# A two-layer hybrid attention trunk: first tile in two token halves, memory's turns moved, two-pass head sums, minus |z| on VectorE

## What is computed

```python
def hybrid_layer(x, mem, ...):
    h = rms_norm(x, ln_g)
    u = einsum('bsd,de->bse', h, w_in)           # q, k, v, z of four branches, f, gate logits
    o_sb = stick_breaking_attention(q_sb, k_sb, v_sb)            # 4 heads of 64
    o_fx = forgetting_attention(rms_norm(q_fx), rms_norm(k_fx), v_fx, log_sigmoid(f + b))
    o_dl = dilated_mixture(rope(rms_norm(q_dl)), rope(rms_norm(k_dl)), v_dl)   # 12 heads
    km, vm = split(einsum('bmd,de->bme', rms_norm(mem, mem_ln_g), w_mem_kv))   # 256 memory tokens
    o_mm = memory_cross_attention(rms_norm(q_mm), rms_norm(km), vm)
    y_b = (o_b * silu(z_b)) @ w_br_b             # for each branch b
    merged = sum over b of sigmoid(gate_b) * y_b
    return x + merged @ w_out
```

## Time and profile before

| | us |
|---|---|
| median of 3 runs | 1352.54 |
| lowest and highest | 1352.37, 1352.62 |
| the profiled execution | 1349.81 |
| its span | 1348.0 |
| TensorE busy in it | 1295.9 |
| mean granted TensorE clock | 0.982 |

### The profile page before, as it was taken

How to read it: one execution, slowest core, us unless ns; L and a number is a source line. 1 busy time by engine, 2 the same in 40 slices (tenths; PEclk the granted TensorE clock), 3 DMA queues, 4 the chain that set the end, 5 groups by cost and what they waited for, 6 DMA issues and landing times. The chain is left out here.

```text
span 1348.0 us, 17624 instructions
## 1 busy us (share of the span) xinstructions
PE 1295.9 (96%) x6138; PEld 1022.6 (76%) x6138; DVE 559.3 (41%) x929; ACT 684.1 (51%) x1257; POOL 694.3 (52%) x571
## 2 busy tenths in 40 slices
PE   7998989998999999999999999999999999999998
PEld 6777868875677788887887787787666778888876
DVE  5896253354341322223349945334542313222221
ACT  6665333586444645454456643248745355544531
POOL 4687322364242476777457863125633325767662
PEclk9999989999999999999999998999999999999999
DMA  7545311122222244444364452112222223444432
GB/s 229 157 105 135 97 39 32 48 63 54 54 59 53 66 107 113 107 113 113 98 166 128 118 131 58 39 40 60 59 55 56 55 55 88 114 104 110 105 115 86
DMA packets 209888, 120.79 MB, mean 90 GB/s; under 512 B 9736, under 2 KB 200328, under 8 KB 209800
## 3 DMA queue, kind: packets, MB, share of 16 engines
q1 hardware_dynamic: 209800, 119.66, 33.8%
HBM read 107.04 MB, written 6.29 MB: 84 GB/s over the span
## 5 line engine op out<-in xcount | busy, mean ns | idle before, releaser
L1699 POOL TENSOR_TENSOR w_lo<-w_raw,w_hi 128x512 fp32r<-128x512 f32 (+1 forms) x400 | 498.1, 1251 | 596.0 <-ACT w_hi L1173 547.3
L765 PE MATMUL dense<-h_hi,w_hi 128*128 128x512 f32 x1168 | 496.4, 425 | 5.3 <-POOL w_lo L1699 2.8
L765 PE MATMUL dense<-h_lo,w_hi 128*128 128x512 f32 x1168 | 461.9, 395 | 0.0
L765 PE MATMUL dense<-h_hi,w_lo 128*128 128x512 f32 x1152 | 454.5, 395 | 0.0
L765 PEld LDWEIGHTS dense<-h_hi,w_hi 128*128 128x128 f32 x1168 | 223.0, 191 | 70.1 <-issue 15.8
L1173 ACT ACTIVATE w_hi<-w_raw 128x512 fp32r<-128x512 f32 (+1 forms) x401 | 231.8, 585 | 67.5 <-PE dense L765 66.3
L765 PEld LDWEIGHTS dense<-h_lo,w_hi 128*128 128x128 f32 x1168 | 223.4, 191 | 48.5 <-issue 9.7
L765 PEld LDWEIGHTS dense<-h_hi,w_lo 128*128 128x128 f32 x1152 | 219.7, 191 | 48.5
L1461 DVE TENSOR_TENSOR sig<-dense,x_rstd_row 128x512 f32<-128x512 f32 x48 | 33.2, 692 | 207.7 <-issue 118.4
L1226 ACT ACTIVATE sig<-sig 128x512 f32<-128x512 f32 x48 | 30.3, 632 | 123.2 <-DVE sig L1461 123.2
L1463 DVE TENSOR_TENSOR raw<-dense,x_rstd_row 128x512 f32<-128x512 f32 x80 | 54.9, 686 | 80.8 <-PE dense L765 62.4
(11 more groups left out here) (292 smaller groups left out, 2021.1 us busy)
## 6 DMA issues: line engine op xcount, KB each, us to landing
w_raw<-in_w_in SPq DMA_DIRECT2D x292, 256.0 KB, 2.9
w_raw<-in_w_out SPq DMA_DIRECT2D x32, 256.0 KB, 2.9
x_scratch<-v_dil SPq DMA_DIRECT2D x16, 256.0 KB, 3.5
w_raw<-in_w_mem_kv SPq DMA_DIRECT2D x16, 256.0 KB, 2.8
v_dil<-x_scratch SPq DMA_DIRECT2D x16, 256.0 KB, 2.7
turned<-normed SPq DMA_DIRECT2D x48, 64.0 KB, 2.4
inv_den<-o_norm SPq DMA_DIRECT2D x48, 64.0 KB, 2.4
silu_z<-in_mem SPq DMA_DIRECT2D x4, 512.0 KB
```

What stands on the lines that cost most here:

```text
L765: return nc.tensor.matmul(o, lhsT, rhs, start=start, stop=stop, skip_group_check=True)
L1699: pool.tensor_tensor(w_lo[:, g % SPLIT_SLOTS, c], w_raw[:, g % RAW_SLOTS, c], f(w_hi[:, g % SPLIT_SLOTS, c]), ALU.subtract).then_inc(w_lo_ ...
```

## The change

- The first dense tile of the program runs as eight k-tiles over tokens 0 to 255, then eight over 256 to 511 (`first_tile`), and VectorE's `first_low` and `x_place` are reordered: four lows of half 0, the copies of x tiles 2 and 3, the other four lows of half 0, the eight of half 1.
- `mem_square` moves to the end of the first group; `mem_scale` and the four turns go to the start of the second. Its order is now four full value tiles, then mk 0, v 4, mk 1, v 5, mv 0, z 0, mv 1, z 1. The scaling is done by ScalarE.
- All normed tiles have the square in two parts and two fp32r passes, and they are held back for at least one more tile.
- The second turn of the dilated maxima goes to bank `A1`.
- VectorE forms -|z| as min(-z, z) right behind its copy; ScalarE's Abs goes.
- A stick-breaking step of key tile j is followed by 3 - j free places; six free places at the end of the third group go.

```diff
-ROOM_AT_END = 12
+ROOM_AT_END = 6
@@ scores(SB)
+                if s < len(order):
+                    yield from [("room",)] * (TT - 1 - order[s][1])
@@ dense
-                if waiting[2] and waiting[2][-1].rope:
+                if waiting[2] and waiting[2][-1].normed:
                     add("low", waiting[2][-1])
...
-                while len(waiting[2]) >= lag and not (waiting[3] and waiting[3][-1].rope and waiting[2][0].rope):
+                while waiting[2] and len(waiting[2]) >= max(lag, 1 + waiting[2][0].normed) and not (waiting[3] and waiting[3][-1].rope and waiting[2][0].rope):
@@ plan_layer
-    dense([new(kind, DIL, i) for kind in "qk" for i in range(6)], [("room",), ("x_sum",)] + [("room",)] * 6
-          + [("mem_square",), ("mem_scale",)] + [("mem_t", c) for c in range(4)] + [("room",)] * 2, lag=2)
-    dense([new(*t) for v, t in enumerate((("mk", MM, 0), ("mk", MM, 1), ("mv", MM, 0), ("mv", MM, 1)))
-           for t in (("v", DIL, v), t)] + [new("v", DIL, i) for i in (4, 5)] + pair_of("z", DIL), lag=2)
+    dense([new(kind, DIL, i) for kind in "qk" for i in range(6)], [("room",), ("x_sum",)] + [("room",)] * 13 + [("mem_square",)], lag=2)
+    dense([new(*t) for t in (("v", DIL, 0), ("v", DIL, 1), ("v", DIL, 2), ("v", DIL, 3), ("mk", MM, 0), ("v", DIL, 4),
+                             ("mk", MM, 1), ("v", DIL, 5), ("mv", MM, 0), ("z", DIL, 0), ("mv", MM, 1), ("z", DIL, 1))],
+          [("mem_scale",), ("room",)] + [("mem_t", c) for c in range(4)] + [("room",)] * 18, lag=2)
@@ rings
-                turn_users += [(("max", DIL, 0), max_kept, DIL), (("max", DIL, 1), max_ready, DIL)]
+                turn_users.append((("max", DIL, 0), max_kept, DIL))
+                out_users[2].append((("max", DIL, 1), max_ready, DIL))
@@ square_parts
-            return [part[:, square_ring.slot(t.n), :] for part in (og_dil_hi, og_dil_lo)]
+            i = square_ring.slot(t.n)
+            if t.rope or t.kind == "mk":
+                return [part[:, i, 0:t.width] for part in (og_dil_hi, og_dil_lo)]
+            return [part[:, 4 + i, :] for part in (dq_hi, dq_lo)]
@@ TensorE
+                def first_tile():
+                    for u in range(2):
+                        c = slice(u * MEM, (u + 1) * MEM)
+                        for kt in range(KT):
+                            half, i = divmod(kt, HALF)
+                            if u == 0 and i == 0:
+                                pe.wait_ge(w_lo_ready, half + 1)
+                            pe.wait_ge(first_h_lo[u], kt + 1)
+                            part = slice(i * P, (i + 1) * P)
+                            last = three(dense_bank[0][:, c], w_hi[:, half, part], w_lo[:, half, part],
+                                         h_hi[:, kt, c], h_lo[:, kt, c], u == 0 and kt == 0, u == 1 and kt == KT - 1)
+                            if u == 1 and i == HALF - 1:
+                                last.then_inc(w_used, 1)
...
-                        if t.rope:
-                            pe.wait_ge(*square_lo_ready.of(t.n))
-                            hi, lo = square_parts(t)
-                            mm(o, rc(HEADSUM), hi, start=True)
-                            last = mm(o, rc(HEADSUM), lo, stop=True)
-                        else:
-                            pe.wait_ge(*squared.of(t.n))
-                            last = mm(o, f(rc(HEADSUM)), square[:, square_ring.slot(t.n), 0:t.width], start=True, stop=True)
+                        pe.wait_ge(*square_lo_ready.of(t.n))
+                        hi, lo = square_parts(t)
+                        mm(o, rc(HEADSUM), hi, start=True)
+                        last = mm(o, rc(HEADSUM), lo, stop=True)
...
-                            wait(pe, turn_ring.before(("max", b, order)))
+                            wait(pe, (turn_ring, out_ring[2])[order].before(("max", b, order)))
@@ ScalarE
+                    elif kind == "mem_scale":
+                        act.wait_ge(*mem_rstd.of("exp"))
+                        for i in range(2):
+                            act.activation(mem_tok[:, i, :], mem_tok[:, i, :], ACT.Copy, scale=mem_ms[:, i:i + 1])\
+                                .then_inc(mem_scaled.sem, 1)
...
-                        act.activation(t_, sbz[n % 4][:, w], ACT.Abs).then_inc(z_abs.sem, 1)
                         act.wait_ge(*z_abs.of(key))
-                        act.activation(t_, t_, ACT.Exp, scale=-1.0).then_inc(z_exp.sem, 1)
+                        act.activation(t_, t_, ACT.Exp).then_inc(z_exp.sem, 1)
@@ VectorE
-            first_low(0, 0)
-            first_low(0, 1)
+            for kt in range(HALF):
+                first_low(0, kt)
             x_place(2)
             x_place(3)
             dve.wait_ge(x_placed, 8)
+            for kt in range(HALF, KT):
+                first_low(0, kt)
             for kt in range(KT):
-                if kt >= 2:
-                    first_low(0, kt)
                 first_low(1, kt)
...
                         dve.tensor_copy(sbz[n % 4][:, w], R[score_ring.slot(s)][:, w]).then_inc(z_kept.sem, 1)
+                        dve.wait_ge(*z_kept.of(key))
+                        z = sbz[n % 4][:, w]
+                        dve.scalar_tensor_tensor(out=sbt[n % 2][:, w], in0=z, scalar=-1.0, in1=z, op0=ALU.mult, op1=ALU.min)\
+                            .then_inc(z_abs.sem, 1)
```

More of the change, by code:

```diff
@@ L866, in _ @@
                         t, half, i = s[1:]
+                        if (l, t.n) == (0, 0):
+                            if (half, i) == (0, 0):
+                                first_tile()
+                            continue
                         g = global_item(t.items[half])
@@ L1234, in _ @@
                                        ACT.Square).then_inc(squared.sem, 1)
-                        if t.rope:
-                            act.wait_ge(*squared.of(t.n))
-                            act.activation(square_parts(t)[0], square[:, square_ring.slot(t.n), :], ACT.Copy)\
-                                .then_inc(square_hi_ready.sem, 1)
+                        act.wait_ge(*squared.of(t.n))
+                        act.activation(square_parts(t)[0], square[:, square_ring.slot(t.n), 0:t.width], ACT.Copy)\
+                            .then_inc(square_hi_ready.sem, 1)
                     elif kind == "post2" and s[1].normed:
@@ L1422, in _ @@
                                 .then_inc(out_copied[0], 1)
-                    elif kind == "mem_scale":
-                        dve.wait_ge(*mem_rstd.of("exp"))
-                        for i in range(2):
-                            dve.tensor_scalar(mem_tok[:, i, :], mem_tok[:, i, :], mem_ms[:, i:i + 1], None, ALU.mult)\
-                                .then_inc(mem_scaled.sem, 1)
                     elif kind == "mem_t":
@@ L1515, in _ @@
                         dve.wait_ge(*square_hi_ready.of(t.n))
-                        dve.tensor_tensor(lo, square[:, square_ring.slot(t.n), :], f(hi), ALU.subtract)\
+                        dve.tensor_tensor(lo, square[:, square_ring.slot(t.n), 0:t.width], f(hi), ALU.subtract)\
                             .then_inc(square_lo_ready.sem, 1)
@@ L1610, in _ @@
                             natural = lambda ap: ap.rearrange("p (u r) -> p r u", r=STRIDE)
[L1611 removed]
+                            dve.tensor_tensor(natural(negmax_r[0:NH, :]), A1[0:NH, :].rearrange("p (r u) -> p r u", r=STRIDE),
                                               natural(normed[0:NH, :]), ALU.min).then_inc(max_ready.sem, 1)
```

12 lines of the change are left out of this document (5 added, 7 removed).

## The result

The changed kernel takes 1342.64 us (median of 4 runs, 1339.64 to 1343.98) beside 1352.58 us before: a ratio of 0.9924, 95% interval 0.9910 to 0.9939. It is 9.9 us faster; the forecast of 1313 promised 39.6, and the range ended at 1326. So 29.6 us are missing. The profiled run took 1343.98 us, with a span of 1341.9.

A forecast was written before the change was run, and what follows sets the result against it. The prediction took TensorE's work at its granted clock plus its waits as the bound. Terms of 40.6 us less 1.4 for new waits gave 39.2: 1310.6 for the profiled run, 1313 for the median, range 1303 to 1326.

The forecast's parts named there:

- the head sums' term: Two passes save 6.2 us of matmuls; added copies and subtractions are covered by the lag, which removes 1.6 us of wait.
- the price of the closer rooms: Closer rooms in the dilated columns and later q and k of the third group bring new waits, taken as 1.4 us.
- signs of being wrong: VectorE's chain to negmax_r no shorter, half-clock units still thirteen, or new waits in the value tiles above 5 us.
- First tile: Splitting the first dense tile in two parts lets TensorE start earlier: 1.3 us, bounds 0 to 1.7.
- Memory: Key and value tiles: 12.7 us of waits go, plus 4.7 us from three half-clock units; scaling done 0.4 us before turn 0.
- Maxima: Second turn of the dilated maxima no longer waits for VectorE's copy: 5.2 us in layer 0, 3.7 in layer 1.
- Stick-breaking: Waits for a probability and dk_lo go, net 3.5 us; with the half-clock unit at 976, 5.2 us.
- (3): Rival: the eight half-clock units dropped or hidden turn up elsewhere, six fully paid: 1323 us; chance 0.12.
- (1): Rival: new waits in the value tiles, GpSimd's queue 3 us a layer over its cover, scaling late by 1: 1321; chance 0.14.
- (2): Rival: minus |z| on VectorE contends with GpSimd's reads and lengthens each of 16 steps by 2.3 us: 1355; chance 0.03.
- (4): Rival: more is gained, as four half-clock units after the dilated columns move away (6.6 us): 1306; chance 0.11.
- (5): Rival: waits are not where the change acts, for instance A1 is taken when the maxima come: 1322; chance 0.05.

The follow-up runs named there:

- best three: The kernel before with first tile, memory and maxima together, without the sticks' and head sums' parts: 1328.14 us.
- p_max: The kernel before with only the second turn of the first branch's maxima put into bank A1: 1343.60 us.
- p_stick: The kernel before with only the smaller rooms of the stick-breaking steps and minus |z| on VectorE: 2.3 us slower.
- p_heads: The kernel before with only the head sums in two passes and the lag of the normed tiles: 1362.15 us.
- b_heads: The best three with two passes and lag, Forgetting's gate tiles set between its query tiles, and memory's maxima turned 3 places later: 1331.18 us.
- p_absz: The kernel before with only minus |z| moved from ScalarE to VectorE, rooms as they were: 1352.72 us.
- p_memory: The kernel before with only the value tiles' group order, memory's turns among them and the scaling on ScalarE: 15.8 us faster.
- a_pop: The changed kernel with only one normed tile's second step taken per tile: 1.8 us faster than the changed kernel.
- b_pass_absz: The best three with two passes, no lag, and minus |z| on VectorE: 5.5 us faster than the same without minus |z| there (1350.84 us).
- w_long: The best three with TensorE made to wait at eight places for the gate's last step: 1368.2 us.
- b_memt1: The best three with memory's turns one place further behind the scaling: 1327.52 us.

## Why the prediction was wrong

The step that failed most is the overlap in the head sums' term: the added copies and subtractions, and the lag that was to cover them, were put at nothing, and they cost more than the cheaper matmuls gave (9.7 us lost instead of 7.8 gained). Next is the price of the closer rooms, 1.4 us for all, in the sticks' part (4.9 lost instead of 5.2 gained). Two of the prediction's own signs of being wrong came: more than 5 us of new waits in the value tiles (5.1 for the scaling alone), and a count of half-clock units that didn't fall.

The chain of medians adds up to the missing 29.6 us within 0.3: first tile, memory and maxima 24.5 instead of 27.6 (3.1 short), the sticks' part -4.9 instead of 5.2 (10.1), the head sums' part -9.7 instead of 7.8 (17.5), less the reserve of 1.4 that the forecast had kept back.

**What bounds the kernel.** Right: TensorE is busy for 96 to 97% of the span before, after and in the best three. That work, clock and waits add up to the span is so by construction and shows nothing more.

**First tile.** Not shown to be 1.3. The pair of profiles gives 1.36 us (31.40 to 30.04 for the first head sum), but this mark moves from run to run. In the nine kernels with the old first tile it lies between 29.99 (p_max) and 33.56 us, with a half-clock unit inside the tile in six of them; in the eleven with the new one between 29.61 and 30.34, with no unit. The medians are 31.82 and 29.95. So a gain is likely, and what sets it apart is mostly the unit, which the term didn't have. It wasn't run alone, and memory and maxima alone add up to 25.0 us, more than the 24.5 of the best three, so the medians show nothing of it.

**Memory.** Near in size, 15.8 against 17.4, and partly by luck: of the 12.7 us of waits that were to go, 7.1 went, and what made up the rest isn't shown. The step "0.4 us before TensorE's turn 0" failed: it was 2.5 us after, in both layers. ScalarE's scaling began at 94.43, where TensorE wanted the turn at 94.1, because the square ahead of it waited 1.15 us for VectorE's raw tile; VectorE is late in the key tiles even without memory's work. I had counted ScalarE's free time, not what stood in its queue.

**Maxima.** Right in size in its own kernel: 9.2 against 8.9. In the changed kernel the stretch of the earlier trace rows was 22.15 us against my 20.7, since the first turn came too early (1.21 and 0.70 us of wait on negmax), which is the sticks' rooms.

**Stick-breaking.** The step at the sticks' end was right in its own kernel (3.6 against 3.5), and the failing step was the sentence on closer rooms: I priced it at 1.4 us for all and spread it nowhere, while the first turn of the maxima alone waits 2.1 in p_stick, and the runs with the rooms alone have a granted clock of 0.980 on the mean beside 0.985. In the changed kernel the end of the sticks failed too: its waits on dk_lo and probs are 7.5 us, against 8.9 before. Timeline on VectorE and ScalarE:

```profile
304.13 0.67 ACT L1268 ACTIVATE square<-turn,small 128x512 f32<-128x512 f32 x1
304.83 0.63 ACT L1271 ACTIVATE square<-square 128x512 f32<-128x512 f32 x1
```

```profile
305.58 0.75 DVE L1523 SCALAR_TENSOR_TENSOR normed<-raw,small,square 128x512 f32<-128x512 f32 x1 [3.13 <-ACT square L1271]
306.24 1.78 DVE L1691 SCALAR_TENSOR_TENSOR v_dil<-v_dil 128x512 f32<-128x512 f32 x1
```

VectorE waits 3.13 us for the exp of a lagged tile's head sum, and the sticks' plus, due long before, goes after it, and takes 1.78 us. TensorE then waits 2.17 us for dk_lo and 1.26 for the probability behind it. The lag of one part and the rooms of the other meet there; each alone has these two smaller (1.5 and 1.1 in p_stick, 0.82 and 0.78 in p_heads, which has a third of 2.75), and without the head sums' part the sum of 7.5 is 5.5.

**Head sums.** The term fits as a price of matmuls: work fell by 2.8 to 7.4 us in the six pairs of kernels with and without the passes, 6.2 forecast, though work scatters by as much between kernels with the same matmuls. The price of a missing cover came near, 16 times 1.3 is 20.8 us and the passes without the lag were 20.6 slower, but by another way: eight waits of up to 3.3 us, and the clock. What failed is the sentence "their cover is the new lag of a tile". I let the lag cover the split and named what it removes (a wait of 1.6), and did not ask who else is moved by it. Now a head sum stands right ahead of a value tile's turn, and at memory's maxima a head sum's logarithm comes behind the next tile's square on ScalarE; both turns use bank T. Those two waits are 11.0 us in p_heads, with units at 344, 368, 1010 and 1034 right behind them, none of which the lag alone has. b_heads, on the best three and with 2.5 us of them left, loses 3.0 instead of 9.7. The rest went in smaller waits elsewhere.

**Half clock.** I counted eight units to go and none to come, with rival (3) at 0.12. Two more are there than before. A list of the new waits would have given some of them: those at 310, 358, 754, 969, 993 and 1017 stand at waits of 2.17 to 2.89 us. It wouldn't have given those at 160, 191, 201, 232, 846, 857 and 881, which have no wait of 2 us ahead, and the waits of 2.54 us at 96.66 and 2.58 at 334.81 have no unit.

**Rivals.** (1) came in part: w_lo and the scaling wait 8.2 us in the changed kernel, but the bound in the changed kernel was the scaling, and GpSimd's queue showed only when I moved the turns. (2) fell as a price: minus |z| is slow, 1.06 us in the median of the changed kernel, and costs at most about 1 us. The page of the Trainium skill that I set beside it (SBUF — State Buffer, Who interferes with whom) says that a VectorE instruction with two SBUF inputs contends with a GpSimd instruction that reads SBUF. The trace of the changed kernel agrees as far as it goes: six of its eight minus |z| of 128x384 ran with GpSimd idle for all but 0.03 us and took 0.56 us, the other two ran beside GpSimd all along and took 1.22 and 1.52. In p_absz one of them took 0.56 us beside a GpSimd instruction, so it doesn't hold for each. (3) is the nearest to what happened, with the units at new waits. (4) and (5) fell: units came instead of going, and nothing waits for bank A1. No rival had the lag in it.

## What to carry to other kernels

When a change adds a lag to cover something, follow each later instruction to its new place: which other step now uses the same bank there, and what stands ahead of it in each engine's queue. An instruction that is ready can still wait for the one before it, and an engine's free time says nothing of that. Price a new wait by more than its length, since it can bring the half clock: here added waits of 1.5 us cost 1.9 each and those of 3.3 us cost 5.0. Before a difference of some us between two profiles is put down to a cause, see where each profiled execution stands among all executions of its kernel. And run parts of a change alone: three of five parts here made 24.5 us, and the other two took 14.5 back.

## What the runs showed of the hardware

Eight added waits of 1.50 us brought no half-clock unit, eight of 3.28 us brought eight, seven of the waits having one and one of these two. The waits of 2.3 to 2.6 us in these traces are mixed: 2.33 in the lag's kernel is followed by a unit at 322, 2.32 in the kernel before by none. Long ones are not certain either: of 30 waits of 3.2 us or more in the twenty profiles (without the first, for the loads), 26 have a unit that begins within 2 us of their end, and four have none (3.49 at 177 in p_memory, 3.50 at 366 in a_pop, 3.28 at 997 in b_pass_absz, 3.29 at 1202 in w_long). The pairs of units in the dilated columns (211 and 242 before, 199 and 230 in the best three), with no wait ahead of them, came in layer 0 of every kernel but one: b_memt1 has only 220 of them. In layer 1 there are more exceptions (p_absz has only 894). What sets them is open, and so is why b_memt1 loses 6 us less to the clock than the best three and is no faster.
